# Transposing u as float32r from a copy in a hybrid decoder block

## The chip, the cores and the metric

The kernel runs on one core of a Trainium2 chip. The metric is the device time of one execution in microseconds (us). Before the change the median of three runs is 1527.35 us (1527.03 to 1528.93). Engines are named as the profile names them: PE is TensorE, PEld its loading of weights, DVE is VectorE, ACT is ScalarE, POOL is GpSimd, SP is SyncE; SPq and ACTq are the instructions by which SP and ACT issue transfers.

## What is computed

The reference is one decoder block on 256 tokens with a model width of 2048, in float32. A normalised x is projected to the inputs of two branches, a gated DeltaNet and a dilated window attention; they are mixed by gates, projected and added to x. Then comes the part that the change touches, a feed-forward layer of width 8192 with a squared ReLU:

```python
h = _rmsnorm(x, ln2_w[l])
u = jax.nn.relu(jnp.einsum("bsd,df->bsf", h, w_ff1[l]))
x = x + jnp.einsum("bsf,fd->bsd", jnp.square(u), w_ff2[l])
```

## The kernel before

Every large product is made in the rounded 32-bit kind (F32R, float32r), in which PE streams a column faster than in plain float32. To keep the precision of float32 each operand is split into a high part, rounded to that kind, and a low part, the remainder; three matmuls (high by high, low by high, high by low) stand for one product.

The weights come from HBM in tiles of 1024 KB, issued by SP into a ring of four buffers, raw. ACT makes the high part of each half tile (a piece, 128 x 1024 numbers; `split`, line 940) into hi, DVE the low part (line 1369) into lo. Both work four pieces ahead of PE (`ahead`, lines 943 and 1372) and fit other steps in at numbered places between the splits: step m is done ahead of the split of piece m + 4. PE frees a piece with piece_used when its last matmul has read it.

A group (`group`, line 474) multiplies eight pieces with the two halves of the tokens, 96 matmuls, into the two banks acc[:, 0] and acc[:, 1]. Its matmuls come in 16 places of six; dicts name steps that PE takes behind a place. `after={1: ...}` is behind the fourth place, that is behind 24 matmuls.

The feed-forward layer is done in two halves of 4096 columns of w_ff1. In each half eight groups (g = 0 to 7) make 512 columns of u each. At the end of a group ACT reads both banks through ReLU and the row scale into the tile us (lines 973 and 977), and DVE squares us in place (`u_square`, line 1928), which raises u_squared. The second product needs u with its columns on the partitions. So while PE works on the next group, behind its 24th matmul, PE turns us (`u_turn`, line 838): eight transposes of 128x128 by the identity through `turn` (line 503) into two banks of PSUM, tbv. For g = 7 the turn stands in the second product instead, behind its first three pieces. ACT copies the turned u to u_hi (`u_hi_step`, step 2), DVE makes u_lo (`u_lo_step`, step 2). For groups 0, 3 and 5 of a half (SEVENS) ACT also copies the turned u to u_copy, POOL makes four sums from it, and these are split to high and low parts too.

Each engine takes its instructions in order, and the engines are coordinated by semaphores (ev[...]). The groups 2 to 7 of a half are a loop on PE (`pe.Fori(2, 8)`), whose turn has g as a register.

The functions and what calls them:

Of the kernel before, what the change touches and what calls it, by code (L numbers as in the profile page):

```python
# [32 lines left out]
F32 = mybir.dt.float32  # L33
F32R = mybir.dt.float32r
I32 = mybir.dt.int32
ALU = mybir.AluOpType
ACT = mybir.ActivationFunctionType
AX_X = mybir.AxisListType.X

P = 128  # L40
TT = 2
D = 2048
KC = D // P
N = 512
# [44 lines left out]
    n_kd n_rv n_diff n_min n_decay n_kk n_lt0 n_LT n_aq0 n_aq n_Ls n_P n_Pc n_c0 n_c1 n_S2 n_S3 n_Ma n_Mb n_Ra n_Rb n_U n_u n_w n_vn  # L89
    n_wT n_S n_o0 n_Sc n_ws n_qs n_vn1 n_qe n_o1 n_oc n_sq n_nss n_nl n_nr n_on n_out d_turned d_hi d_lo  # L90
    m_mixed x_back e_turned e_hi e_lo e_square u_squared u_turned u_hi u_lo stored c_gate angles ab_act
    ab_vec g_vec n_init uc_made s_made s_hi s_lo t_made c_done c_first c_second c_copied""".split()


def build_block(nc, x, positions, inv_freq, ln1_w, w_in, conv_w, a_log, dt_bias, gdn_norm_w, w_gdn_proj,
                q_norm_w, k_norm_w, w_swa_proj, w_out, ln2_w, w_ff1, w_ff2, out):
    ctx = ExitStack()
    with ctx:
        KB = 1024

        def sb(name, shape, dt, at):
            return nc.alloc_sbuf_tensor_at(name, shape, dt, offset=int(at * KB) + BASE)
# [8 lines left out]
        ident = sb("ident", [P, P], F32, 96)  # L111
# [75 lines left out]
        x1 = sb("x1", [P, TT, D], F32, 144)  # L187
        x_scr2 = sb("x_scr2", [P, D], F32, 192)

        us = sb("us", [P, TT, N], F32, 202)  # L190
        sum2 = sb("sum2", [P, N], F32, 202)
        sum3 = sb("sum3", [P, N], F32, 204)

# [4 lines left out]
        u_copy = sb("u_copy", [P, 4, TT * P], F32, 206)  # L198
# [4 lines left out]
        wk = ctx.enter_context(nc.psum_tensor("wk", [P, 6, N], F32))  # L203
# [3 lines left out]
        tbv = tb.rearrange("p a (b t) -> p (a b) t", t=TT * P)  # L207
# [24 lines left out]
        ev = {n: sem(n) for n in EVENTS}  # L232
# [30 lines left out]
        def piece0(half):  # L263
            return 8 * (QG1 if half else QG0) + MORE_PIECES * half

        def octet0(np_, o):
            return HALF_PIECES // 2 * np_ + sum(OCTET_PIECES[:o])
# [205 lines left out]
        def _(pe):  # L473
# [29 lines left out]
            def turn(src, dst, done):  # L503

                for b in range(4):
                    for t in range(TT):
                        last = pe.transpose(dst[:, b, P * t:P * t + P], src(t, b), ident[:])  # L507
                last.then_inc(done, 1)
# [154 lines left out]
            for gi in range(8):  # L663
                h = gi // 2
                t = gi % 2
# [171 lines left out]

            def u_turn(half, g, first=False):
                def step():
                    pe.wait_ge(ev["u_squared"], g + 8 * half + 1)  # L840
                    if first:
                        if half == 0:
                            pe.wait_ge(ev["e_lo"], 16)
                        else:
                            pe.wait_ge(ev["u_lo"], 8)
                            pe.wait_ge(ev["c_second"], 8)
                    else:
                        pe.wait_ge(ev["u_lo"], g + 8 * half)
                    turn(lambda t, b: us[:, t, P * b:P * b + P], tbv, ev["u_turned"])
                return step  # L850

            def wait_e():
# [66 lines left out]
            for half, (qf, gf) in enumerate(((QF0, GF0), (QF1, GF1))):  # L919
                more = MORE_PIECES * half  # L920
                group(qf, gf, 8, st_hi, st_lo, after={} if half else {1: x_turn(3), 5: wait_e}, more=more,
                      banks_read=(5, 7) if half else None)
                group(qf + 1, gf + 1, 8, st_hi, st_lo, after={1: u_turn(half, 0, True)}, more=more)
                with pe.Fori(2, 8) as g:
                    group(qf + g, gf + g, 8, st_hi, st_lo, after={1: u_turn(half, g - 1)}, more=more)
                for np_ in range(2):
                    for o in range(OCTETS):
                        if o in SEVENS:
                            products(half, np_, o, gf)
                        else:  # L930
                            plain(half, np_, o)
# [3 lines left out]
        def _(act):  # L935
# [104 lines left out]
            for n in range(6):  # L1040
                if n == 0:
                    steps = {1: right_hi(2), 2: right_hi(3), 3: x_sum(0), 4: x_sum(1), 5: sines, 6: x_factor}
# [226 lines left out]
            def x_hi(g):  # L1269
                def step():  # L1270
                    act.wait_ge(ev["e_turned"], g + 1)
                    for b in range(4):
                        act.activation(st_hi[:, 4 * g + b], tbv[:, b], ACT.Copy,
                                       scale=lncol[:, KC + 4 * g + b:KC + 4 * g + b + 1]).then_inc(ev["e_hi"], 1)
                return step
# [15 lines left out]
            def u_hi_step(half, g):  # L1291
                def plain():
                    f(u_hi[g][:], tbv, ACT.Copy, (ev["u_turned"], g + 8 * half + 1), ev["u_hi"])

                def parts():
                    n = len(SEVENS) * half + SEVENS.index(g)
                    act.wait_ge(ev["u_turned"], g + 8 * half + 1)
                    if g:
                        act.wait_ge(ev["s_made"], 4 * n)
                    elif half:  # L1300
                        act.wait_ge(lo_ready, piece0(0) + octet0(1, SEVENS[-1]) + 4)
                    act.activation(u_copy[:], tbv, ACT.Copy).then_inc(ev["uc_made"], 1)
                    act.activation(u_hi[g][:, 0:2], tbv[:, :, 0:P].rearrange("p (c k) t -> p c k t", c=2), ACT.Copy)
                    act.activation(u_hi[g][:, 2], tbv[:, 2:4, P:2 * P], ACT.Copy).then_inc(ev["u_hi"], 1)
                return parts if g in SEVENS else plain

            def s_hi_step(half, g):
                def step():
# [22 lines left out]
            for half, (qf, gf, qnext) in enumerate(((QF0, GF0, QF1), (QF1, GF1, None))):  # L1331
                for g in range(8):
                    steps = {}
                    if half == 0 and g == 0:
                        steps = {1: x_hi(3), 3: x_stats}
                    elif g:
                        steps = {2: u_hi_step(half, g - 1)}
                        if g - 1 in SEVENS:
                            steps[5] = s_hi_step(half, g - 1)
                    if g:  # L1340
                        before = (ev["u_turned"], g + 8 * half)
                    else:
                        before = (ev["c_first"], 2 * SUMS) if half else None
                    ahead(qf + g, 8, steps, more=MORE_PIECES * half,
                          then=(lambda p, half=half: piece(half, p)) if g == 7 else None,
                          read_out=read_out(qf + g, gf + g, 8, lambda t: us[:, t], func=ACT.Relu, scale=rstd2,
                                            before=before, more=MORE_PIECES * half))
                for p, (np_, o, n) in enumerate(pieces_of(half)):
                    if p == 2:
                        u_hi_step(half, 7)()  # L1350
                    if o == SEVENS[-1] and n == 4:
                        copy_first(half, np_)
                    if half and np_ and o == 0 and n == 3:
                        store(slice(0, TT), slice(0, 2 * N), 12)
                    if p + PIECES < HALF_PIECES:
                        piece(half, p + PIECES)
                    elif half == 0:
                        split(qnext, p + PIECES - HALF_PIECES, MORE_PIECES)
# [6 lines left out]
        def _(dve):  # L1365
# [554 lines left out]
            def s_lo_step(half, g):  # L1920
# [2 lines left out]
                        (ev["s_hi"], len(SEVENS) * half + SEVENS.index(g) + 1), ev["s_lo"])  # L1923
                return step

            def u_square(g, n):
                dve.wait_ge(acc_free, 2 * g + 4)
                dve.tensor_tensor(us[:], us[:], us[:], ALU.mult).then_inc(ev["u_squared"], 1)
# [118 lines left out]
            for half, (qf, gf, qnext) in enumerate(((QF0, GF0, QF1), (QF1, GF1, None))):  # L2047
                for g in range(8):
                    steps = {}
                    if half == 0 and g == 0:  # L2050
                        steps = {1: x_lo(3)}
                    elif g:
                        steps = {2: u_lo_step(half, g - 1)}
                        if g - 1 in SEVENS:
                            steps[6] = s_lo_step(half, g - 1)
                    ahead(qf + g, 8, steps, more=MORE_PIECES * half,
                          then=(lambda p, half=half: piece(half, p)) if g == 7 else None,
                          more_steps=(lambda p, half=half: between(half, p - 8)) if g == 7 else None)
                    u_square(gf + g, g + 8 * half)
                for p in range(HALF_PIECES + 1):  # L2060
                    between(half, p)
                    if p + PIECES < HALF_PIECES:
                        piece(half, p + PIECES)
                    elif half == 0 and p < HALF_PIECES:
                        split(qnext, p + PIECES - HALF_PIECES, MORE_PIECES)
# [27 lines left out]
```

## Time and profile before

| what | us |
|---|---|
| median of 3 runs | 1527.35 |
| the profiled execution | 1528.7 |
| its span, first to last instruction | 1526.9 |
| PE busy in the span | 1518.2 |
| DVE busy | 1045.9 |
| ACT busy | 788.6 |
| POOL busy | 74.4 |

The trace is of one execution. A row of the timeline gives the start, the duration, the engine, the line of the kernel, the operation and out<-in by the names of the program; in brackets is how long the engine stood idle before it and which instruction ended that. Durations of matmuls include the way through the array, so the starts tell how fast they follow each other: a row of 0.39 us may be followed by the next 0.23 us later. The columns of groups of rows are explained where a view is first used. DVE squares us eight times between 853.0 and 1012.9 us, for the first half, and eight times between 1200.6 and 1360.4 us, for the second.

### The profile page before, as it was taken

The numbers are of one execution on the slowest core, as the hardware profiler recorded it, in microseconds if no ns is written. First come the engines' busy times: TensorE is split into PE (matmuls) and PEld (weight loads), VectorE is DVE, ScalarE is ACT, GpSimd is POOL, SyncE is SP. The second block draws the span as 40 slices with busy tenths as digits, with TensorE's granted clock in tenths as the row PEclk, the third lists the DMA queues.
The fourth block names the chain that finished last, engine by engine and source line by source line (L and its number), as shares of the span: only waits on it lengthen the run. The fifth ranks groups of instructions, "written<-read, shape, count | busy, mean of one in ns | idle before, by whom it ended". The sixth has DMA issues, their size and how long they took to land.

```text
span 1526.9 us, 18779 instructions
## 1 busy us (share of the span) xinstructions
PE 1518.2 (99%) x7132; PEld 1263.2 (83%) x7132; DVE 1045.9 (68%) x1238; ACT 788.6 (52%) x885; POOL 74.4 (5%) x121
## 2 busy tenths in 40 slices
PE   9999999999999999999999999999999999999999
PEld 7888888888888888888888888888888888888887
DVE  5867635777776877776655555578877555578976
ACT  5554445666654544554444645555554545555543
POOL 5000000000040100100000000000000000000000
PEclk9999999999999999999999999999999999999999
DMA  8455554444554444445655656556556555556662
GB/s 285 167 201 186 193 193 142 162 165 138 166 166 156 146 140 143 144 153 171 243 192 171 192 189 193 182 192 204 197 198 211 183 182 188 191 191 198 217 208 96
DMA packets 140291, 276.08 MB, mean 181 GB/s; under 512 B 7104, under 2 KB 7616, under 8 KB 139968
## 3 DMA queue, kind: packets, MB, share of 16 engines
q1 hardware_dynamic: 138960, 273.05, 54.3%
q10 hardware_dynamic: 1264, 2.13, 0.4%
q8 instruction: 43, 0.70, 0.2%
q14 instruction: 24, 0.20, 0.0%
HBM read 273.06 MB, written 2.10 MB: 180 GB/s over the span
## 4 chain that ended last, share of the span: by engine, by line
PE 95%; DVE 3%; issue 1%; ACT 1%; DMA 0%; SPq 0%; DVEq 0%; ACTq 0%
PE acc L491 65%; PE wk L911 7%; PE acc L911 7%; PE wk L887 5%; PE wk L507 2%; PE acc L887 2%; DVE lo L1369 1%; PE wk L755 1%; PE wk L630 1%; DVE diag L1388 1%; PE wk L603 1%; PE wk L746 1%; PE wk L590 0%; DVE both__109 L1388 0%; ACT hi L940 0%
## 5 line engine op out<-in xcount | busy, mean ns | idle before, releaser
L1369 DVE TENSOR_TENSOR lo<-raw,hi 128x1024 fp32r<-128x1024 f32 x384 | 469.6, 1228 | 348.4 <-ACT hi L940 339.4
L940 ACT ACTIVATE hi<-raw 128x1024 fp32r<-128x1024 f32 x383 | 404.9, 1058 | 429.8 <-PE acc L491 422.8
L491 PE MATMUL acc<-hi,st_hi 128*128 128x512 f32 x1312 | 524.4, 400 | 2.2 <-DVE gates L1685 1.6
L491 PE MATMUL acc<-lo,st_hi 128*128 128x512 f32 x1312 | 511.7, 390 | 0.0
L491 PE MATMUL acc<-hi,st_lo 128*128 128x512 f32 x1312 | 511.0, 389 | 0.0
L491 PEld LDWEIGHTS acc<-hi,st_hi 128*128 128x128 f32 x1312 | 246.7, 188 | 51.9 <-issue 3.3
L491 PEld LDWEIGHTS acc<-lo,st_hi 128*128 128x128 f32 x1312 | 246.2, 188 | 52.2
L491 PEld LDWEIGHTS acc<-hi,st_lo 128*128 128x128 f32 x1312 | 246.8, 188 | 48.1 <-issue 1.0
L1317 ACT ACTIVATE hi<-raw 128x1024 fp32r<-128x1024 f32 x116 | 122.9, 1061 | 136.0 <-PE wk L911 116.4
L1934 DVE TENSOR_TENSOR lo<-raw,hi 128x1024 fp32r<-128x1024 f32 x116 | 141.1, 1222 | 53.0 <-ACT hi L1317 50.5
L911 PE MATMUL acc<-hi,u_hi 128*128 128x512 f32 x160 | 62.2, 389 | 0.0
L911 PE MATMUL acc<-hi,u_lo 128*128 128x512 f32 x160 | 62.2, 389 | 0.0
L911 PE MATMUL acc<-lo,u_hi 128*128 128x512 f32 x160 | 62.2, 389 | 0.0
L911 PE MATMUL wk<-hi,u_hi 128*128 128x512 f32 x160 | 62.2, 389 | 0.0
L911 PE MATMUL wk<-hi,u_lo 128*128 128x512 f32 x160 | 62.2, 389 | 0.0
L911 PE MATMUL wk<-lo,u_hi 128*128 128x512 f32 x160 | 62.2, 389 | 0.0
L1934 DVE TENSOR_TENSOR lo<-t_sums,hi 128x1024 fp32r<-128x1024 f32 x48 | 58.2, 1223 | 5.6 <-ACT hi L1317 1.3
L1317 ACT ACTIVATE hi<-t_sums 128x1024 fp32r<-128x1024 f32 x48 | 50.7, 1061 | 12.3 <-PE acc L887 6.3
L491 PE MATMUL acc<-hi,mix_hi 128*128 128x512 f32 x128 | 50.2, 392 | 0.0
L491 PE MATMUL acc<-lo,mix_hi 128*128 128x512 f32 x128 | 49.9, 390 | 0.0
L491 PE MATMUL acc<-hi,mix_lo 128*128 128x512 f32 x128 | 49.8, 389 | 0.0
L887 PE MATMUL wk<-hi,u_hi 128*128 128x512 f32 x120 | 46.9, 391 | 0.0
(296 smaller groups left out, 1709.0 us busy)
## 6 DMA issues: line engine op xcount, KB each, us to landing
raw<-in_w_ff SPq DMA_DIRECT2D x128, 1024.0 KB, 5.2
raw<-in_w_in SPq DMA_DIRECT2D x99, 1024.0 KB, 4.9
raw<-in_w_out SPq DMA_DIRECT2D x16, 1024.0 KB, 5.1
raw<-in_w_gdn_proj SPq DMA_DIRECT2D x8, 1024.0 KB, 5.0
raw<-in_w_swa_proj SPq DMA_DIRECT2D x4, 1024.0 KB, 5.1
x_tok<-in_x SPq DMA_DIRECT2D x2, 1024.0 KB, 9.5
x<-in_x SPq DMA_DIRECT2D x1, 2048.0 KB, 7.6
raw<-in_w_in SPq DMA_DIRECT2D x2, 512.0 KB, 8.0
```

Of the source, the lines that this page charges most:

```text
L491: last = pe.matmul(acc[:, t], w[:, k0 + 2 * m + kk, P * t:P * t + P], v[:, (i + more) % PIECES, kk, :], start=m == 0 and kk == 0 and a == ...
L507: last = pe.transpose(dst[:, b, P * t:P * t + P], src(t, b), ident[:])
L603: last = pe.matmul(wk[:, 2 + g * nk // N, g * nk % N:g * nk % N + nk], qc[:, g, P * t:P * t + P], swa_qk[:, 1, HS * g + h, 0:nk], start=Tr ...
L630: last = pe.matmul(wk[:, 4, 0:P], pt[:, P * b:P * b + P], swa_v[:, kt, at:at + P], start=b == 0, stop=b == NG * (t + 1) - 1)
L746: last = pe.matmul(blk(W[0], h), Ls[:, l % 2, h, :], diag[:, 1, h, :], start=True, stop=True)
L755: last = pe.matmul(blk(W[3], h), diag[:, 0, h, :], Pc[:, h, :], start=True, stop=True)
L887: last = pe.matmul(banks[name], w[:, kk, :], v[:, slot, kk, :], start=o == 0 and kk == 0 and a == 0, stop=alone and o == SEVENS[-1] and kk ...
L911: last = pe.matmul(banks[t], w[:, 2 * m + kk, P * t:P * t + P], v[:, slot, kk, :], start=begins and m == 0 and kk == 0 and a == 0, stop=o ...
L940: act.activation(hi[:, (i + more) % PIECES], raw[:, i // 2 % RAW, 2 * (i % 2):2 * (i % 2) + 2, :], ACT.Copy)\
L1317: act.activation(hi[:, (piece0(half) + p) % PIECES], src, ACT.Copy).then_inc(hi_ready, 1)
L1369: dve.tensor_tensor(lo[:, (i + more) % PIECES], raw[:, i // 2 % RAW, 2 * (i % 2):2 * (i % 2) + 2, :], hi[:, (i + more) % PIECES].bitcast(F ...
L1934: dve.tensor_tensor(lo[:, a % PIECES], src, hi[:, a % PIECES].bitcast(F32), ALU.subtract)\
```

## The change

A second tile us_r of the rounded kind and a rounded copy of the identity are added. In 14 of the 16 groups (g = 0 to 6 of both halves) ACT issues a transfer that copies the squared us, bit by bit, to us_r; PE waits until it has landed (us_moved) and turns us_r by the rounded identity as that kind, in place of turning us. The two groups with g = 7 are turned as before. ACT issues the transfer at its step 1, between the splits of pieces 4 and 5 of the next group, behind a wait for u_squared. Beside that, in the first group of the first half PE also turns us plainly into two other banks of PSUM; DVE takes the difference of the two turns, multiplies it by 1e8 and adds it to x1 (`same`, at DVE's step 4), and PE waits for that at the end of the group, ACT before it next writes u_copy. The rounded identity is made once on ACT at step 5 of the first group. The events us_moved, ident_r_made and us_same are added to the list.

```diff
@@ -188,6 +188,8 @@
         x_scr2 = sb("x_scr2", [P, D], F32, 192)
 
         us = sb("us", [P, TT, N], F32, 202)
+        us_r = sb("us_r", [P, TT, N], F32R, 214)
+        ident_r = sb("ident_r", [P, P], F32R, 201)
         sum2 = sb("sum2", [P, N], F32, 202)
         sum3 = sb("sum3", [P, N], F32, 204)
 
@@ -837,6 +839,7 @@
 
             def u_turn(half, g, first=False):
                 def step():
+                    moved = isinstance(g, int) and g == 7
                     pe.wait_ge(ev["u_squared"], g + 8 * half + 1)
                     if first:
                         if half == 0:
@@ -846,7 +849,20 @@
                             pe.wait_ge(ev["c_second"], 8)
                     else:
                         pe.wait_ge(ev["u_lo"], g + 8 * half)
-                    turn(lambda t, b: us[:, t, P * b:P * b + P], tbv, ev["u_turned"])
+                    if moved:
+                        turn(lambda t, b: us[:, t, P * b:P * b + P], tbv, ev["u_turned"])
+                        return
+                    if first and half == 0:
+                        pe.wait_ge(ev["ident_r_made"], 1)
+                    pe.wait_ge(ev["us_moved"], 16 * g + 112 * half + 16)
+                    view = tbv.bitcast(F32R)
+                    for b in range(4):
+                        for t in range(TT):
+                            last = pe.transpose(view[:, b, P * t:P * t + P], us_r[:, t, P * b:P * b + P], ident_r[:])
+                    last.then_inc(ev["u_turned"], 1)
+                    if first and half == 0:
+                        turn(lambda t, b: us[:, t, P * b:P * b + P],
+                             wk[:, 2:4, :].rearrange("p a (b t) -> p (a b) t", t=TT * P), ev["us_same"])
                 return step
 
             def wait_e():
@@ -921,6 +937,8 @@
                 group(qf, gf, 8, st_hi, st_lo, after={} if half else {1: x_turn(3), 5: wait_e}, more=more,
                       banks_read=(5, 7) if half else None)
                 group(qf + 1, gf + 1, 8, st_hi, st_lo, after={1: u_turn(half, 0, True)}, more=more)
+                if half == 0:
+                    pe.wait_ge(ev["us_same"], 4)
                 with pe.Fori(2, 8) as g:
                     group(qf + g, gf + g, 8, st_hi, st_lo, after={1: u_turn(half, g - 1)}, more=more)
                 for np_ in range(2):
@@ -1299,10 +1317,21 @@
                         act.wait_ge(ev["s_made"], 4 * n)
                     elif half:
                         act.wait_ge(lo_ready, piece0(0) + octet0(1, SEVENS[-1]) + 4)
+                    if g and not half:
+                        act.wait_ge(ev["us_same"], 4)
                     act.activation(u_copy[:], tbv, ACT.Copy).then_inc(ev["uc_made"], 1)
                     act.activation(u_hi[g][:, 0:2], tbv[:, :, 0:P].rearrange("p (c k) t -> p c k t", c=2), ACT.Copy)
                     act.activation(u_hi[g][:, 2], tbv[:, 2:4, P:2 * P], ACT.Copy).then_inc(ev["u_hi"], 1)
                 return parts if g in SEVENS else plain
+
+            def make_ident_r():
+                act.activation(ident_r[:], ident[:], ACT.Copy).then_inc(ev["ident_r_made"], 1)
+
+            def move_us(half, g):
+                def step():
+                    act.wait_ge(ev["u_squared"], 8 * half + g + 1)
+                    act.dma_start(us_r[:].bitcast(F32), us[:]).then_inc(ev["us_moved"], 16)
+                return step
 
             def s_hi_step(half, g):
                 def step():
@@ -1332,9 +1361,9 @@
                 for g in range(8):
                     steps = {}
                     if half == 0 and g == 0:
-                        steps = {1: x_hi(3), 3: x_stats}
+                        steps = {1: x_hi(3), 3: x_stats, 5: make_ident_r}
                     elif g:
-                        steps = {2: u_hi_step(half, g - 1)}
+                        steps = {1: move_us(half, g - 1), 2: u_hi_step(half, g - 1)}
                         if g - 1 in SEVENS:
                             steps[5] = s_hi_step(half, g - 1)
                     if g:
@@ -1922,6 +1951,17 @@
                     tt_(u_lo[g][:, 3:7], u_sums[:], u_hi[g][:, 3:7].bitcast(F32), ALU.subtract,
                         (ev["s_hi"], len(SEVENS) * half + SEVENS.index(g) + 1), ev["s_lo"])
                 return step
+
+            def same():
+
+                dve.wait_ge(ev["us_same"], 1)
+                dve.wait_ge(ev["s_made"], 4)
+                dve.tensor_copy(u_copy[:], wk[:, 2:4, :].rearrange("p a (b t) -> p (a b) t", t=TT * P)).then_inc(ev["us_same"], 1)
+                dve.wait_ge(ev["us_same"], 2)
+                dve.tensor_tensor(u_copy[:], tbv, u_copy[:], ALU.subtract).then_inc(ev["us_same"], 1)
+                v = x1[:, 0, 0:2 * N].rearrange("p (b t) -> p b t", b=4)
+                dve.wait_ge(ev["us_same"], 3)
+                dve.scalar_tensor_tensor(out=v, in0=u_copy[:], scalar=1e8, in1=v, op0=ALU.mult, op1=ALU.add).then_inc(ev["us_same"], 1)
 
             def u_square(g, n):
                 dve.wait_ge(acc_free, 2 * g + 4)
@@ -2051,6 +2091,8 @@
                         steps = {1: x_lo(3)}
                     elif g:
                         steps = {2: u_lo_step(half, g - 1)}
+                        if half == 0 and g == 1:
+                            steps[4] = same
                         if g - 1 in SEVENS:
                             steps[6] = s_lo_step(half, g - 1)
                     ahead(qf + g, 8, steps, more=MORE_PIECES * half,
```

## Rows read from the trace of the kernel before

**Rows 1.** The page: busy time by engine, and two of the costliest groups.
```profile
PE 1518.2 (99%) x7132; PEld 1263.2 (83%) x7132; DVE 1045.9 (68%) x1238; ACT 788.6 (52%) x885; POOL 74.4 (5%) x121
...
L940 ACT ACTIVATE hi<-raw 128x1024 fp32r<-128x1024 f32 x383 | 404.9, 1058 | 429.8 <-PE acc L491 422.8
...
L491 PEld LDWEIGHTS acc<-hi,st_hi 128*128 128x128 f32 x1312 | 246.7, 188 | 51.9 <-issue 3.3
```

**Rows 2.** Waits of PE: who for whom, us in total, times, longest.
```profile
PE acc L491 <- DVE gates L1685: 1.6, 4, 0.8
PE acc L514 <- POOL ones L383: 1.2, 1, 1.2
...
PE acc L491 <- issue: 0.3, 1, 0.3
```

**Rows 3.** Busy time by engine in one period; then granted clock, DMA share, GB/s.
```profile
core 0: us, PE busy (x) PEld busy (x) DVE busy (x) ACT busy (x) POOL busy (x), PEclk, DMA share, GB/s
850.00:872.66 22.66, 22.66 (x105) 18.84 (x104) 13.09 (x12) 12.26 (x14) 2.99 (x4) 1.00 0.64 202
```

**Rows 4.** Timeline of PE, around the first turn of u.
```profile
855.21 0.40 PE L491 MATMUL acc<-lo,st_hi 128*128 128x512 f32 x1
855.44 1.04 PE L507 MATMUL wk<-ident,us 128*128 128x128 f32 x8
856.24 0.47 PE L491 MATMUL acc<-hi,st_hi 128*128 128x512 f32 x1
856.55 0.39 PE L491 MATMUL acc<-hi,st_lo 128*128 128x512 f32 x1
```

**Rows 5.** Tile us: duration ns min/median/max, first and last start.
```profile
L507 PEld LDWEIGHTS wk<-ident,us x128: 138/140/143, 855.2 to 1361.2; 128*128 128x128 f32 x128
L507 PE MATMUL wk<-ident,us x128: 270/273/328, 855.4 to 1361.3; 128*128 128x128 f32 x128
...
L1928 DVE TENSOR_TENSOR us<-us x16: 1216/1219/1220, 853.0 to 1359.2; 128x1024 f32<-128x1024 f32 x16
```

**Rows 6.** Timeline of DVE in the first period.
```profile
853.01 1.22 DVE L1928 TENSOR_TENSOR us<-us 128x1024 f32<-128x1024 f32 x1
...
867.24 1.23 DVE L1369 TENSOR_TENSOR lo<-raw,hi 128x1024 fp32r<-128x1024 f32 x1 [2.85 <-ACT hi L940]
```

**Rows 7.** Timeline of ACT in the first period.
```profile
854.34 1.06 ACT L940 ACTIVATE hi<-raw 128x1024 fp32r<-128x1024 f32 x1 [2.50 <-PE acc L491]
855.71 1.06 ACT L940 ACTIVATE hi<-raw 128x1024 fp32r<-128x1024 f32 x1 [0.31 <-PE acc L491]
```

**Rows 8.** Timeline of ACT and its queue at the first store.
```profile
1444.70 1.06 ACT L1317 ACTIVATE hi<-t_sums 128x1024 fp32r<-128x1024 f32 x1 [0.30 <-PE acc L887]
1444.73 0.41 ACTq L1329 DMA_DIRECT2D out_x<-x  x1
```

**Rows 9.** Issues of transfers: count, KB each, median us to landing.
```profile
raw<-in_w_ff SPq DMA_DIRECT2D x128, 1024.0 KB, 5.2
...
raw<-in_w_in SPq DMA_DIRECT2D x2, 512.0 KB, 8.0
out_x<-x ACTq DMA_DIRECT2D x1, 1024.0 KB, 6.4
out_x<-x ACTq DMA_DIRECT2D x4, 256.0 KB, 2.3
...
rows<-in_ln_w SPq DMA_DIRECT2D x2, 8.0 KB, 1.8
```

**Rows 10.** Busy time by engine, behind the place of the new transfer.
```profile
854.40:858.10 3.70, 3.70 (x22) 3.15 (x21) 2.45 (x2) 3.39 (x5) 0.34 (x1) 1.00 0.88 285
```

**Rows 11.** Groups of PE by form: shapes, count, busy us, mean ns, idle before.
```profile
L491 PE MATMUL acc<-hi,st_lo 128*128 128x512 f32 x1312 | 511.0, 389 | 0.0
...
L590 PE MATMUL wk<-e_even,ones 128*128 128x512 f32 x8 | 3.8, 591 | 0.0
...
L649 PE MATMUL wk<-fold,ab_cols 32*128 32x16 f32 x4 | 0.6, 263 | 0.0
```

**Rows 12.** Timeline of PE at L649, products with 16 columns.
```profile
233.14 0.61 PE L649 MATMUL wk<-fold,ab_cols 32*128 32x16 f32 x4
```

**Rows 13.** Timeline of PE at the start of the kernel.
```profile
1.21 3.78 PE L514 MATMUL acc<-ones 128*128 128x256 f32 x8 [1.21 <-POOL ones L383]
...
14.34 1.89 PE L514 MATMUL acc<-ones 128*128 128x256 f32 x8
```

More of the change, by code:

```diff
@@ L91 @@
     m_mixed x_back e_turned e_hi e_lo e_square u_squared u_turned u_hi u_lo stored c_gate angles ab_act
-    ab_vec g_vec n_init uc_made s_made s_hi s_lo t_made c_done c_first c_second c_copied""".split()
+    ab_vec g_vec n_init uc_made s_made s_hi s_lo t_made c_done c_first c_second c_copied us_moved ident_r_made us_same""".split()
 def build_block(nc, x, positions, inv_freq, ln1_w, w_in, conv_w, a_log, dt_bias, gdn_norm_w, w_gdn_proj,
```

## The prediction

> **What bounds the kernel now.** I read the page first, then PE's waits, then the order of time around one turn of u. The page shows PE busy for 99% of the span [rows 1]. The list of PE's waits has seven rows, from 1.6 down to 0.3 us in all [rows 2]: no engine and no transfer holds PE up. So time is saved only by taking work off PE, and whatever PE stands still for is lost, unless it can be caught up later; it can't, because PE never waits for the others.
>
> In the stage that the change touches, the reader is to see one period: from 850.00 to 872.66 PE is busy throughout [rows 3]. It holds a group of 96 matmuls and one turn. The turn starts at 855.44, one matmul behind it at 856.24 and the next at 856.55 [rows 4]; less one matmul's 0.23 (855.44 less 855.21), turn and the switch back take 1.11 - 0.23 = 0.88 us, 0.11 us for each of the eight pieces. The matmuls then have (22.66 - 0.88) / 96 = 0.227 us each. The 128 pieces and 16 squares of u last the same in every group [rows 5], so one group stands for all 14 that change.
>
> **The new wait, the term that decides.** DVE squares u from 853.01 for 1.22 us, to 854.23 [rows 6]. Now PE could turn it at once, and comes to it only at 855.44: the square is 1.2 us early. In the change a copy to us_r comes between, and PE waits for its landing at the same place in its order, behind the 24th matmul. PE takes its instructions in order, so the turn and the 72 matmuls behind it stand, and with them u_hi on ACT, u_lo on DVE and the splits that wait for freed pieces.
>
> When is the copy issued? On ACT it is queued behind the split that starts at 854.34 [rows 7]; the square is done by then. A store that ACT issued in such an order began 0.03 us after the activation ahead of it had started, and took 0.41 us of issue [rows 8]. So: issue at 854.37. The stall is 854.37 + L - 855.44 = L - 1.07 us, L being the time from issue to landing of 512 KB (128 x 1024 x 4 bytes).
>
> No row shows a transfer from SBUF to SBUF, so L is bounded from both sides, all from [rows 9]. Lower end: 8 KB took 1.8 us, and nothing landed sooner. Upper end: the only two of 512 KB took 8.0 us, at the start of the kernel, where several loads are queued together. Between them 256 KB, stored at the end of the run, took 2.3 us, a load of 1024 KB 5.2 us, and 1024 KB stored from ACT beside running loads 6.4 us. A straight line from 256 KB at 2.3 to 1024 KB at 6.4 gives 3.7 us for 512 KB. But the copy isn't alone: from 854.40 to 858.10 the DMA engines are 0.88 busy and move 285 GB/s [rows 10]. If the second 256 KB gets half of that, it takes 262144 / 142.5e3 = 1.8 us, and L = 2.3 + 1.8 = 4.1. I take 4.0, nearest to these two: stall 2.93 us a turn, 14 turns, **+41.0 us**. The ends: L = 1.8 gives 0.73 x 14 = 10.2 us, L = 8.0 gives 6.93 x 14 = 97 us.
>
> The Trainium skill (DMA: Bandwidth & Descriptors, Anatomy of one DMA) puts a transfer at about 2.0 us fixed and its bytes at 436 GB/s, fitted on another issue path; for 512 KB an estimate of 3.2 us. The traced 256 KB in 2.3 us lies close to it (its figure: 2.6), the 1024 KB in 6.4 us beside loads does not (its figure: 4.4). By it the stall would be 2.1 us and the term 30 us.
>
> **The turn as the rounded kind.** The records of a plain 32-bit product with 512 columns last 591 ns, those of the rounded kind 389 ns [rows 11]: 202 ns less for 512 columns, so 50 ns for 128. If all of that were gained, a turn would lose 8 x 0.05 = 0.40 us, 14 turns 5.7 us. Against it: four records with only 16 columns, but 128 columns of weights, take 0.61 us [rows 12], one of them 0.26 in the mean [rows 11], and so start (0.61 - 0.26) / 3 = 0.117 us apart. That is no less than the 0.11 us of the turn's pieces with 128 columns. So the spacing is set by the weights' load, not by the columns that stream, and the rounded kind's load is no shorter: 188 ns a record [rows 1], against 140 in the turn of u [rows 5]. I take 0 us. The other end: the rounded kind with few columns could need two such load-and-product pairs, as a plain 32-bit product does (L649: two products in the code, four records [rows 11]); 0.11 us more for each of 112 pieces, +12.3 us.
>
> **The group that compares.** PE turns the first group a second time, plainly: **+0.9 us**, once. The rest lies off the path. DVE's three operations on 128x1024 take about 1.22 us each, as the square does, 3.7 us in all, ahead of the split at 867.24, before which DVE was idle for 2.85 us [rows 6]: that split ends about 1 us later. PE needs it only in the next group, which begins at 872.66. The sums of POOL, for which DVE waits there, are 2.99 us of work [rows 3] behind ACT's copy of the turned u, over before DVE comes to that place. PE's wait at the end of the group is met at some 864.4 + 3.7 = 868.1, 4.5 us early; without that cover it would cost up to 3.7 us, once. The rounded identity is one small activation, on an engine that is busy for 12.26 of the period's 22.66 us [rows 3].
>
> **What else moves.** On ACT the copy's issue (0.41 us, to 854.78) stands ahead of the split at 855.71, which waits for PE anyway [rows 7]: 0.9 us of cover, so nothing. SP's queue isn't passed, but its loads share the DMA engines: 0.5 MB more in a group on a share of 0.64 [rows 3]. Of the 429.8 us that ACT stood idle ahead of splits, PE ended 422.8 [rows 1]: the loads come early, and a load that lands 1 to 2 us later costs nothing; if that cover were gone, it would be those 1 to 2 us a group, some 20 us.
>
> **Sum.** 41.0 + 0 + 0.9 = 41.9 us. The profiled execution took 1528.7 us (span 1526.9); 1528.7 + 41.9 = 1570.6. The median of the runs is 1.35 us below it: 1569 us.
>
> **Rivals.**
> (a) The transfer is quick: L of 2.3 to 3.3, as 256 KB alone, or on the line from there to the load of 5.2 us. For it: SBUF at both ends, no far memory. Against: the load that is moving. Stalls of 1.2 to 2.2 us: 1545 to 1559. Chance 0.20.
> (b) The transfer is slow: L of 5 to 6.4, as the store beside loads. For it: that row; against: half its bytes. Stalls of 3.9 to 5.3 us: 1583 to 1603. Chance 0.12.
> (c) The stalls cost PE its clock. Eight warm-up matmuls take 3.78 us at the start of the kernel, the same eight 1.89 us from 14.34 on [rows 13]: PE began at the lower of its two levels (1.2 against 2.4 GHz) and rose behind activity. In the stage that changes, the granted clock is 1.00, the higher level [rows 3, 10]. No row shows a fall, since nothing in the run before leaves PE waiting for more than 1.2 us. If each stall had the turn and the 24 matmuls behind it at half speed, that is up to 0.88 + 5.44 = 6.3 us more a turn: from 1570 up to 1657. Chance 0.12. The Trainium skill (TensorE: Matmul & The Clock Gate, HAM oscillation) has such falls behind waits for DMA between bursts of matmuls, so it speaks against this change beyond my sum.
> (d) The other side: not slower. The one mechanism is that the copy is hidden and the turn gains: L at most 1.07 us, so that PE never waits, and pieces at half their time. Then -5.7 + 0.9: 1523. It decides at a stall of 0.34 us a turn (4.8 / 14), L = 1.4. Against it: no landing under 1.8 us. Chance 0.03.
> That the turn gains nothing from the rounded kind is in my forecast already; a gain would shift each case by less than 6 us.
>
> **Numbers.** The forecast (L of 3.3 to 5.0: 1559 to 1583) has 0.53. The range that holds 8 of 10 takes in most of (a), (b) and the near part of (c), and the turn's own -6 to +12: 1549 to 1603. About 0.2% (3 us) is what a measurement of this kernel can tell from no change. Only (d), or a landing near 1.4 us, gives less: faster 0.015, same 0.015, slower 0.97.
>
> **What would show it.** In the profile after: idle time of PE ahead of the turn, some 2.9 us, 14 times, ended by a transfer that writes us_r; copies on ACT's queue with about 4.0 us to landing, issued 1.1 us ahead of the turn's old place; a period near 25.6 us instead of 22.66; pieces of the turn still 0.11 us apart; matmuls behind each stall at 0.227 us. Wrong would be: PE not idle at the turn, pieces at 0.06 us, matmuls of 0.43 us behind the stalls, or ACT's splits waiting for loads.

## The result and the profile after

The changed kernel takes 1635.24 us (median of 4 runs, 1634.55 to 1636.51), against 1528.14 before (4 runs): 1.0704 times as long, 95% interval 1.0691 to 1.0717. The prediction was 1569 us with a range of 1549 to 1603. The direction was right; the loss is 107 us where some 41 were forecast.

The profiled execution took 1635.71 us, its span is 1634.0. The page of the changed kernel, with the lines that answer to [rows 1] and [rows 9]; the line numbers moved with the added code (line 940 of before is 958, line 507 is 509, the new turn is line 861):

```profile
PE 1552.7 (95%) x7140; PEld 1286.1 (79%) x7140; DVE 1050.1 (64%) x1241; ACT 790.4 (48%) x886; POOL 73.3 (4%) x121
...
PEclk9999999999999999999998998999999998999999
...
L958 ACT ACTIVATE hi<-raw 128x1024 fp32r<-128x1024 f32 x383 | 405.0, 1058 | 461.7 <-PE acc L493 454.7
...
L861 PE MATMUL wk<-ident_r,us_r 128*128 128x128 f32 x112 | 17.3, 329 | 71.7 <-DMA us_r<-us 71.7
...
us_r<-us ACTq DMA_DIRECT2D x14, 512.0 KB, 6.3
```

The span grew by 107.1 us. Two rows of the page hold nearly all of it: PE stood idle for 71.7 us ahead of the new turn, and PE's busy time grew from 1518.2 to 1552.7, by 34.5 us, although the work on it grew by one turn only. ACT's idle time ahead of its splits is still ended by PE, 454.7 of 461.7 us: the loads stay early.

Where the busy time grew is seen in the order of time on PE, the view of [rows 4], in the second changed group:

```profile
891.96 1.25 PE L861 MATMUL wk<-ident_r,us_r 128*128 128x128 f32 x8 [5.22 <-DMA us_r<-us]
893.02 0.76 PE L493 MATMUL acc<-hi,st_hi 128*128 128x512 f32 x1
893.57 0.63 PE L493 MATMUL acc<-hi,st_lo 128*128 128x512 f32 x1
894.00 0.63 PE L493 MATMUL acc<-lo,st_hi 128*128 128x512 f32 x1
```

The matmuls behind the wait start 0.43 us apart (894.00 less 893.57), where before it was 0.227. The granted clock by stretches, the view of [rows 3], says the same for the first changed group: it is the third number from the end of a row, 0.50 being the lower level, 1.2 GHz, and 1.00 the higher one, 2.4 GHz. The first row holds the turn and the second, plain turn of the compare, the second row the slow matmuls behind them.

```profile
861.00:863.65 2.65, 2.61 (x17) 2.64 (x17) 0.00 (x0) 1.34 (x2) 0.24 (x1) 0.50 0.74 269
863.65:866.00 2.35, 2.35 (x8) 1.87 (x7) 1.02 (x2) 0.45 (x2) 2.27 (x4) 0.51 0.05 17
866.00:880.00 14.00, 14.00 (x63) 11.59 (x62) 9.49 (x8) 5.77 (x6) 0.33 (x1) 1.00 0.23 75
```

The periods say what it costs: from the turn at 891.96 to the next one at 921.85 are 29.9 us, to that at 952.26 30.4, against 22.66 before. Of the 7.2 to 7.8 us more, 5.1 to 5.2 are the wait, and 2.1 to 2.5 the slow turn and the slow matmuls behind it.

### The profile page after: what moved, and what is told of

It is laid out like the page before. It is cut to its first block, busy times and chain, and to the rows that moved or that the text cites. A ratio compares the mean times of both kernels' runs of the same rounds, so it can differ in the third digit from the quotient of the medians.

```text
span 1634.0 us, 18828 instructions
## 1 busy us (share of the span) xinstructions
PE 1552.7 (95%) x7140; PEld 1286.1 (79%) x7140; DVE 1050.1 (64%) x1241; ACT 790.4 (48%) x886; POOL 73.3 (4%) x121
## 4 chain that ended last, share of the span: by engine, by line
PE 89%; DMA 6%; DVE 3%; issue 1%; ACT 1%; SPq 0%; ACTq 0%; DVEq 0%
PE acc L493 62%; PE wk L927 7%; PE acc L927 7%; DMA us_r<-us 5%; PE wk L903 5%; PE acc L903 2%; PE wk L509 2%; PE wk L861 1%; DVE lo L1398 1%; PE wk L757 1%; PE wk L632 0%; PE wk L605 0%; DVE diag L1417 0%; PE wk L748 0%; PE wk L592 0%
## 5 line engine op out<-in xcount | busy, mean ns | idle before, releaser
L958 ACT ACTIVATE hi<-raw 128x1024 fp32r<-128x1024 f32 x383 | 405.0, 1058 | 461.7 <-PE acc L493 454.7
L493 PE MATMUL acc<-hi,st_hi 128*128 128x512 f32 x1312 | 536.9, 409 | 2.6 <-DVE gates L1714 1.6
L493 PE MATMUL acc<-hi,st_lo 128*128 128x512 f32 x1312 | 522.0, 398 | 0.0
L493 PE MATMUL acc<-lo,st_hi 128*128 128x512 f32 x1312 | 521.2, 397 | 0.0
L493 PEld LDWEIGHTS acc<-hi,st_hi 128*128 128x128 f32 x1312 | 254.1, 194 | 54.8 <-issue 3.7
L493 PEld LDWEIGHTS acc<-lo,st_hi 128*128 128x128 f32 x1312 | 253.0, 193 | 55.1
L493 PEld LDWEIGHTS acc<-hi,st_lo 128*128 128x128 f32 x1312 | 254.0, 194 | 50.3 <-issue 1.0
L861 PE MATMUL wk<-ident_r,us_r 128*128 128x128 f32 x112 | 17.3, 329 | 71.7 <-DMA us_r<-us 71.7
L861 PEld LDWEIGHTS wk<-ident_r,us_r 128*128 128x128 f32 x112 | 14.8, 180 | 77.6 <-DMA us_r<-us 66.2
L927 PE MATMUL wk<-hi,u_hi 128*128 128x512 f32 x160 | 62.2, 389 | 0.0
```

Of the source, the lines that this page charges most:

```text
L493: last = pe.matmul(acc[:, t], w[:, k0 + 2 * m + kk, P * t:P * t + P], v[:, (i + more) % PIECES, kk, :], start=m == 0 and kk == 0 and a == ...
L861: last = pe.transpose(view[:, b, P * t:P * t + P], us_r[:, t, P * b:P * b + P], ident_r[:])
L927: last = pe.matmul(banks[t], w[:, 2 * m + kk, P * t:P * t + P], v[:, slot, kk, :], start=begins and m == 0 and kk == 0 and a == 0, stop=o ...
L958: act.activation(hi[:, (i + more) % PIECES], raw[:, i // 2 % RAW, 2 * (i % 2):2 * (i % 2) + 2, :], ACT.Copy)\
```

## The experiments

Every ratio below is against the kernel before, run on the same chip in the same session; the comparing group is in none of the nine kernels. Code is cut at "...".

**1. The copy and the wait without the rounded turn.** The lines are set against the changed kernel.

```diff
-  view = tbv.bitcast(F32R)
-  ... pe.transpose(view[:, b, ...], us_r[:, t, ...], ident_r[:]) ...
+  turn(lambda t, b: us[:, t, P * b:P * b + P], tbv, ev["u_turned"])
```

> The copy and PE's wait for it stay, but the turn reads us plainly, and the comparing group is out. Theory A (the time went into waiting for the copy and into the lower clock behind the wait): idle of 5.1 to 5.4 us ahead of each of 14 turns stays, matmuls behind it still take 0.43 us, and the turn at the lower clock takes 1.6 us in place of 1.05, so some 7 us more than the changed kernel less its compare of 2.6 us: about 1640 us. Rival B (the turn as the rounded kind is what costs, and brings the clock down): under 1610 us, and no slow matmuls.

Measured: 1636.57 us, ratio 1.0724 (1.0693 to 1.0755). The waits and the order of time on PE, the views of [rows 2] and [rows 4]:

```profile
PE wk L509 <- DMA us_r<-us: 71.9, 14, 5.3
```

```profile
887.69 1.97 PE L509 MATMUL wk<-ident,us 128*128 128x128 f32 x8 [5.06 <-DMA us_r<-us]
889.31 0.77 PE L493 MATMUL acc<-hi,st_hi 128*128 128x512 f32 x1
889.88 0.63 PE L493 MATMUL acc<-hi,st_lo 128*128 128x512 f32 x1
```

Rival B falls: the loss is there whole without a single rounded turn. Theory A's 7 us for the slower plain turn came out as some 4 us, against the fourth run (1632.97); the traces show part of the reason: fewer slow matmuls follow the longer turns, 109 of 0.6 us or more against 129 in the fourth run.

**2. PE kept busy while it waits.**

```diff
+  for n in range(22):
+      pe.matmul(p7, st_hi[:, 0, 0:P], st_hi[:, 0:2, :]..., start=True, stop=True)
   pe.wait_ge(ev["us_moved"], 16 * g + 112 * half + 16)
```

> The changed kernel without its compare, and PE does 22 matmuls of 512 columns into an unused bank (22 x 0.227 = 5.0 us) ahead of its wait for the copy; their result is not used. Theory A: PE is no longer idle, so the clock stays at the higher level and the 30 to 34 us of slow matmuls go, while the 14 waits of 5.1 us stay in another form: 1528 + 14 x 5.1 less a gain of the turn of 0 to 5 us, that is 1595 to 1602 us. Rival B (the rounded turn itself brings the clock down): slow matmuls behind each turn stay and the time is about 1633 us.

Measured: 1602.21 us, ratio 1.0499 (1.0468 to 1.0529), some 31 us less than the run without the 22 matmuls (1632.97), and 0.2 us above the range of theory A. The order of time on PE in this run:

```profile
883.17 5.15 PE L858 MATMUL wk<-st_hi 128*128 128x512 f32 x22
888.47 0.88 PE L863 MATMUL wk<-ident_r,us_r 128*128 128x128 f32 x8
889.19 0.46 PE L493 MATMUL acc<-hi,st_hi 128*128 128x512 f32 x1
```

The 22 matmuls fill nearly all of the wait (seven waits are left, 3.0 us in all, the longest 1.4), and the turn behind them goes on at once, 0.72 us to the next matmul, where it was 1.06 (893.02 less 891.96). No matmul behind the turns takes 0.6 us or more, where 129 did in the fourth run. The granted clock can't be read for this in the profiled execution: its column has 0.95 in every stretch, also far from the turns, while the matmuls keep their 0.227 us; the other execution has 1.00 and took 1601.79 us. By the pace of the matmuls, then, the lower clock is caused by PE standing idle, not by the rounded turn; it costs some 31 us.

**3. The same bytes when nothing else moves.**

```diff
   act.wait_ge(ev["stored"], 16 * 5)
+  act.dma_start(there, x1[:, 0, 0:2 * N]...)          # 512 KB SBUF to SBUF
+  act.dma_start(there[:, 0:2], x1[:, 0, 0:N]...)      # 256 KB SBUF to SBUF
+  act.dma_start(there..., w_1_v[:, 0:2, 0:N])         # 512 KB HBM to SBUF
+  act.dma_start(out_v[:, 0, 0:2 * N], x1[:, 0, 0:2 * N])   # 512 KB SBUF to HBM, each behind a wait
```

> The kernel before, with four transfers issued by ACT one after the other behind its last store, when nothing else moves: 512 KB SBUF to SBUF, 256 KB SBUF to SBUF, 512 KB HBM to SBUF, 512 KB SBUF to HBM. Theory C (the load beside it made the copy slow): the first lands after about 3 us, as 256 KB in 2.3 us would lead one to expect, and the 6.3 us of the changed kernel come from sharing. Rival D (a copy with both ends in SBUF is slow by itself): the first takes 5 us or more though nothing else moves, and more than the third and fourth. The whole run is some 10 to 15 us longer than before; that is the transfers' own time.

Measured, the view of [rows 9]:

```profile
quiet_at<-x ACTq DMA_DIRECT2D x1, 512.0 KB, 3.0
quiet_at<-in_w_ff ACTq DMA_DIRECT2D x1, 512.0 KB, 3.7
out_x<-x ACTq DMA_DIRECT2D x1, 512.0 KB, 2.6
quiet_at<-x ACTq DMA_DIRECT2D x1, 256.0 KB, 2.3
```

512 KB from SBUF to SBUF land after 3.0 us, less than a load of that size (3.7) and a little more than a store (2.6), one transfer of each. Rival D falls: a copy inside SBUF is not slow by itself. What moves beside it is left as the reason for the 3.3 us more in the changed kernel; run 5 tests that.

**4. Without the comparing group.**

```diff
-  if first and half == 0:
-      turn(lambda t, b: us[...], wk[:, 2:4, :]..., ev["us_same"])
...
-  if half == 0 and g == 1:
-      steps[4] = same
```

> The changed kernel without the comparing group. Theory A: the second turn at the lower clock (1.6 us in the trace) goes and nothing else: 1633 to 1634 us, against 1635 for the changed kernel. Rival E (DVE's three operations and PE's wait at the group's end cost too): 1628 us or less.

Measured: 1632.97 us, ratio 1.0700 (1.0667 to 1.0734). The intervals of this run and of the changed kernel overlap, so its cost isn't settled by the times; it is a few us at most. In the trace of the changed kernel the second turn takes 1.58 us, from 862.07 to 863.65.

**5. The load that stood ahead of the copy, issued behind its landing.** SP's loop over the groups is written out, and one tile in four waits:

```diff
+  if j == 1 and i > 1:
+      sp.wait_ge(ev["us_moved"], 16 * i + 112 * half - 16)
   tile(qf + i, j, w_1_v, 4 * j, ...)
```

> The changed kernel without its compare, and SP issues the load that went out 1 us ahead of the copy only when the copy has landed, for 12 of the 14 copies (groups 0 to 5 of each half; SP's loop over the groups is written out). Theory C (the copy is not shared with the load that is moving, but served behind it): the copy lands after 3.0 us as in the quiet run, the waits fall from 5.1 to about 2.0 us (3.0 less 1.07), 12 x 3.1 = 37 us less waiting; if the clock stays up behind a wait of 2 us, 12 x 2.3 = 28 us more: 1633 - 65 = 1568 us, or 1596 with the clock still falling. Loads land 3 to 4 us later, which no engine notices. Rival F (copy and load share the engines in halves, or the time is set elsewhere): L stays above 5 us and the time above 1620.

Measured: 1569.34 us, ratio 1.0277 (1.0262 to 1.0293). PE's waits, the view of [rows 2], and the copies in this run:

```profile
PE wk L864 <- DMA us_r<-us: 30.4, 14, 5.1
```

```profile
us_r<-us ACTq DMA_DIRECT2D x14, 512.0 KB, 2.9
```

The copy lands after 2.9 us, as in the quiet run, the twelve waits fall to 1.67 to 1.85 us, and the time to what theory C gave (1568). The two copies that were left behind a load (the last of each half) still have waits of 5.06 and 4.78 us: the control stands in the same run. Rival F falls. The clock fell behind both of these, and behind 3 of the 12 short waits (matmuls of 0.63 us behind the turn), so it stayed up in 9 of 12.

**6. The turn one step of 24 matmuls later.**

```diff
-  after={1: u_turn(half, g - 1)}
+  after={3: u_turn(half, g - 1)}
...
-  steps = {1: move_us(half, g - 1), 2: u_hi_step(half, g - 1)}
+  steps = {1: move_us(half, g - 1), 4: u_hi_step(half, g - 1)}
```

> The changed kernel without its compare, and the turn stands behind the 48th matmul of the next group in place of the 24th (5.44 us later), with u_hi and u_lo at step 4 and the steps of the sums at 7. The copy is issued as before. Theory A: issue at 854.4 + 6.3 = 860.7 is just ahead of the new place, 860.8: waits of 0 to 0.3 us, no fall of the clock, 1522 to 1530 us, within 0.3% of the kernel before. Rival B (the rounded turn, or the copy's traffic, costs by itself): above 1540 us.

Measured: 1528.69 us, ratio 1.0007 (0.9998 to 1.0016), 10 runs. PE's waits in this run:

```profile
PE wk L861 <- DMA us_r<-us: 2.5, 6, 0.6
```

```profile
us_r<-us ACTq DMA_DIRECT2D x14, 512.0 KB, 6.4
```

Copies of 6.4 us go on beside the work as before, and the whole loss is gone: six waits of at most 0.6 us are left, and no matmul behind a turn is slow. So the copy's traffic and its issue on ACT cost nothing that shows, at most the 1 or 2 us that the rounded turn may have given back; the copy's price is the place at which PE waits for it.

**7. The rounded turn without a copy.** A second name of the rounded kind stands for the place of us, in all 16 groups:

```diff
+  us_r = sb("us_r", [P, TT, N], F32R, 202)
...
-  turn(lambda t, b: us[:, t, ...], tbv, ev["u_turned"])
+  turn(lambda t, b: us_r[:, t, ...], tbv, ev["u_turned"], ident_r)
```

> No copy and no compare: a second name of the rounded kind for the place of us, read by all 16 turns of us as that kind. It measures the rounded turn alone at the higher clock. From the run with PE kept busy, a rounded turn takes 0.72 us to the next matmul in place of 0.80: theory G (the load of the weights sets the spacing, the columns hardly count): 16 x 0.1 = 1 to 2 us less, 1524 us against 1525.4. Rival H (the time of a piece halves): 16 x 0.4 = 6 us less, 1519 us.

Measured: 1526.46 us, ratio 0.9983 (0.9974 to 0.9992), 11 runs: by the ratio 2.6 us less (1.2 to 4.0). The tile and the order of time in this run, the views of [rows 5] and [rows 4]:

```profile
L511 PEld LDWEIGHTS wk<-ident_r,us_r x128: 137/140/144, 852.1 to 1355.6; 128*128 128x128 f32 x128
L511 PE MATMUL wk<-ident_r,us_r x128: 221/249/283, 852.3 to 1355.7; 128*128 128x128 f32 x128
```

```profile
852.34 0.80 PE L511 MATMUL wk<-ident_r,us_r 128*128 128x128 f32 x8
852.98 0.46 PE L494 MATMUL acc<-hi,st_hi 128*128 128x512 f32 x1
```

Eight pieces in 0.64 us to the next matmul, where the plain turn has 0.80 (856.24 less 855.44 in [rows 4]). That is between theory G (0.1 us a turn) and rival H (0.4): 0.16 us a turn by the starts, and 2.6 / 16 = 0.16 us by the times.

**8. All turns of the helper.**

```diff
+  x_tok_r, t1_r, stage_r, o_b_r, o_a_r, mixed_r, x1_r, us_r: each a second name of the rounded kind
+  act.activation(ident_a[:], ident[:], ACT.Copy)   # at the start
```

> As the run before, and all other turns that the helper makes (43 turns of eight pieces in all) read their tiles by a second name of the rounded kind; the rounded identity is made at the start by ACT. Theory G: 43 x 0.1 = 4 us less than the kernel before, 1521 us. Rival H: 43 x 0.4 = 17 us less, 1508 us. Rival I (a wait for the identity at the start, or a turn that gates other work, eats it): 1525 us or more.

Measured: 1520.63 us, ratio 0.9951 (0.9938 to 0.9965): 7.5 us less than before, 0.17 us for each of 43 turns. It is 0.5% faster than the kernel before, which its interval leaves clear of no change. Rival I falls; G, with 4 us, was short by half.

**9. The same load, issued 1 us behind the copy instead of 1 us ahead.** The lines are set against run 5.

```diff
-  sp.wait_ge(ev["us_moved"], 16 * i + 112 * half - 16)
+  sp.wait_ge(hi_ready, 8 * (qf + i - 1) + 5 + MORE_PIECES * half)
```

> The changed kernel without its compare, and SP issues the load that stood 1 us ahead of the copy about 1 us behind the copy's issue (when ACT has made the high part of the split that the copy's issue follows), for 12 of the 14 copies. Nothing waits for the copy but PE. Theory C1 (who is issued first is served first): the copy lands after 3.0 to 3.5 us although a load follows at once, waits of 2.0 to 2.5 us and a time of 1565 to 1580 us. Rival C2 (loads of SP's queue are preferred, or both share): L of 4 us or more, waits of 3 us and more, 1585 us or more.

Measured: 1572.94 us, ratio 1.0293 (1.0263 to 1.0323). The copy in this run, the last column of its row being the median to landing:

```profile
us_r<-us ACTq DMA_DIRECT2D x14, 512.0 KB, 3.2
```

A load that follows at once costs the copy 0.2 to 0.3 us; one that stands 1 us ahead costs it 3.3. That is what theory C1 gave, but the contest is short: with nothing else moving, a load's first bytes came 1.0 us behind its issue (run 3, third transfer), so this one could meet only the last 0.5 us of the copy. Issued at 880.43, it moved no byte before 882.0, when the copy's bytes were through. Behind waits of 1.98 to 2.25 us the clock fell in 5 of 12 cases.

## Why the prediction was wrong, step by step

**The landing time L: the step that failed first.** The term of 41.0 us came from "If the second 256 KB gets half of that, it takes 262144 / 142.5e3 = 1.8 us, and L = 2.3 + 1.8 = 4.1". L was 6.3 (5.4 to 6.5). The anchors were right: the copy is issued at 854.44, the stall is L less 1.1 us, and 71.7 / 14 = 5.1 fits 6.3. But copy and load didn't share by halves. A load was on its way when the copy was issued, and the trace of before has it at the same place; these are its rows in before and after, and the copy's:

```profile
853.26 0.37 SPq L298 DMA_DIRECT2D raw<-in_w_ff  x1
...
853.33 0.37 SPq L300 DMA_DIRECT2D raw<-in_w_ff  x1
854.44 0.52 ACTq L1333 DMA_DIRECT2D us_r<-us  x1
```

In the changed kernel, the queues' bytes from 854.6 to 857.8 us are the first line below (q1 is SP's, q10 ACT's; packets, MB, share of the engines), those from 857.8 to 859.4 the two others:

```profile
q1 hardware_dynamic: 367, 0.75, 91.4%
...
q10 hardware_dynamic: 100, 0.40, 61.0%
q1 hardware_dynamic: 141, 0.26, 42.7%
```

For 3.4 us behind its issue the copy moved nothing (3.0 to 3.8 us in the 14 copies); the load issued at 853.33 had the engines to itself. In run 3 the first bytes came some 1.1 us behind the issue, and so they did in the twelve copies of run 5. So 2.0 to 2.8 us of the loss are waiting behind the load; the rest is lost once the copy's bytes move, over some 2 us in place of 1.5, beside the end of that load and the start of the next. Run 5 shows the cause by taking the load away from ahead of the copy (2.9 us), and run 9 by issuing it behind (3.2 us). The rows that I interpolated carried the warning: the store of 6.4 us beside loads ([rows 9]) was read as a slower rate, where it may as well have been a turn in a line. I read rows for the price of a byte and not for when the first byte moves, and gave the copy half of the stretch's 285 GB/s though the row at 853.26 has a load on its way. Why the later transfer isn't mixed in is not settled by these runs.

The Trainium skill's figures in DMA: Bandwidth & Descriptors (Anatomy of one DMA) give an estimate of 3.2 us for these bytes, by a fit made on another issue path; run 3 has 3.0. It comes close for the transfer alone; with a load ahead 6.3 us were measured.

**The clock: a term put at nothing, a rival that came true.** The sum has no term for the clock; rival (c) had a chance of 0.12, held low on the one ground that no row of before showed a fall. With waits of 5.1 us it happened behind all 14. Its size was some 31 us (run 2 against run 4), 2.2 us a turn, well under the 6.3 us that I had set as the end: the slow stretch covers the turn and 6 to 11 matmuls (counted in run 4), not 24. The two errors hang together: the clock fell behind every wait of 3.9 us or more (46 of 46, in the changed kernel and runs 1, 4, 5 and 9), behind waits of 1.67 to 2.25 us in 8 of 24 cases (runs 5 and 9), and behind waits of up to 1.40 us in none (runs 2 and 6). So at the 2.9 us that I forecast, which no run has, a fall was to be expected in a part of the cases at least, and by these counts a chance of 0.12 for it was low. One reading of that rival is weaker than it looks: the slow start in [rows 13] is known by the doubled time alone, since the clock column has 1.00 there too (1.21 to 5.00 us). The Trainium skill (TensorE: Matmul & The Clock Gate, HAM oscillation) has this fall behind waits for DMA between bursts, and the trace agrees: granted clock 0.50 behind the wait.

**The rounded turn.** I took 0 us from a spacing of 0.117 us at 16 columns and concluded that the weights' load sets it. It doesn't in a turn: the load of the rounded turn has 140 ns a record, as the plain turn's ([rows 5]), not the 188 of [rows 1], and the pieces start 0.08 us apart. The gain is 0.16 to 0.17 us a turn (runs 7 and 8), inside the bounds of 0 to 0.40. Behind a wait it is less: the turn of run 2 has 0.72 us to the next matmul, 0.08 less than the plain one. In the changed kernel some 1 to 2 us may have been gained and can't be seen beside the loss.

**The comparing group.** 0.9 us forecast; its second turn took 1.58 us, at the lower clock. The rest of it was hidden, as said: DVE is through with its three operations at 876.50, and no wait of PE for them is among the eight kinds of wait that the trace of the changed kernel has.

**What was right.** PE waits at the turn's old place, 14 times, for the copy; the copy's issue beside the split costs ACT nothing (854.44 against the split's 854.42); SP's loads land later at no cost that shows (run 6); nothing is caught up, because PE has no slack. Run 5 took the 1569 us of the forecast, but by other terms, 30.4 us of waiting and the clock's loss behind five turns: that agreement is chance. The new sum by measured terms: 71.7 us of waiting and 34.5 us of longer busy time (1.6 of it the compare, nearly all the rest the lower clock, which run 2 prices at some 31) are 106 of the 107 us.

## What to carry to other kernels

Price a new transfer on the critical path by what stands ahead of it on the DMA engines, not by its bytes alone: look up which load is issued just before it, and when the first byte can move. When the engine that bounds the kernel waits, count the slow stretch behind the wait as well. If a transfer has to be there, put its consumer a few microseconds later in the order, where the same transfer cost nothing that shows (run 6); and ask first whether it is needed at all, since a second name for the same bytes did the work of the copy here.

## What the runs showed of the hardware

Two transfers from different queues did not share the engines evenly here: 512 KB took 3.0 us alone, 3.2 us with a load issued 1 us later, 6.3 us with a load issued 1 us earlier. A copy inside SBUF (3.0 us) landed sooner than a load of its size from HBM (3.7 us), and a store to HBM sooner than both (2.6 us), one transfer of each. A turn of the rounded kind gains a fifth (0.64 against 0.80 us to the next matmul), far from the half that the prediction's estimate from [rows 11] would allow. At the lower clock the rounded turn took 1.06 us and the plain one 1.58, 0.13 and 0.20 us a piece.
